# 64 places for experts 0 to 3 (nine blocks for ten), gates applied as results leave PSUM, and a reordered opening

## The reference

```python
for i in range(DEPTH):                                   # 4
    sh1, sc1, g1, sh2, sc2, g2 = adaln(c or c_ctx, w_mod[i], b_mod[i])
    x = x + g1 * mixer(rmsnorm(x, norm_mix[i]) * (1 + sc1) + sh1)
    x = x + g2 * moe(rmsnorm(x, norm_ffn[i]) * (1 + sc2) + sh2)
y = rmsnorm(x, final_norm)

def moe(h, ...):          # 16 experts in 4 groups, 1024 -> 256 -> 1024 each
    s = sigmoid(h @ w_router)        # the best group, its two best experts
    w = s[idx] / sum(s[idx])
    return sum_k w_k * (silu(h @ w_gate[e_k]) * (h @ w_up[e_k])) @ w_down[e_k]
```

## Time and profile before

| | |
|---|---|
| median of 3 runs | 1591.02 us (1586.55 to 1597.87) |
| profiled execution | 1586.19 us, its span 1584.4 us |
| TensorE busy | 1431.5 us (90%) |
| VectorE busy | 555.1 us (35%) |
| ScalarE, GpSimd busy | 372.8 us (24%), 226.8 us (14%) |
| bytes moved | 417.21 MB, 263 GB/s over the span |
| mean granted TensorE clock | 0.969 |

### The profile page before, as it was taken

The page is one execution under the profiler, slowest core; times in us unless marked ns, Lnnn a source line. Parts: engine busy times, 40 slices in busy tenths (PEclk is TensorE's granted clock), DMA queues, the critical chain, the costliest instruction groups (busy, mean ns, idle before and its releaser), DMA issues.

```text
span 1584.4 us, 26599 instructions
## 1 busy us (share of the span) xinstructions
PE 1431.5 (90%) x10752; PEld 854.6 (54%) x10752; DVE 555.1 (35%) x1362; ACT 372.8 (24%) x985; POOL 226.8 (14%) x304
## 2 busy tenths in 40 slices
PE   3999998998998998999889999989989999969983
PEld 1876685332776685333564456753337766853331
DVE  0235524211656525211622343342115256252115
ACT  0205522111214512111210342211112046121111
POOL 0100022111122022111100000222111000221112
PEclk9999998999999999999989999999999999979997
DMA  9898238999978238999857403489998870239992
GB/s 325 294 318 280 74 114 329 337 420 416 331 276 241 87 134 322 343 421 418 284 207 241 115 28 123 168 320 351 421 415 309 288 284 18 109 128 328 422 389 104
DMA packets 122788, 417.21 MB, mean 263 GB/s; under 512 B 13659, under 2 KB 55614, under 8 KB 98086
## 3 DMA queue, kind: packets, MB, share of 16 engines
q1 hardware_dynamic: 95414, 345.08, 58.0%
q0 software_dynamic: 20304, 66.47, 12.7%
q10 hardware_dynamic: 6944, 3.91, 0.8%
HBM read 389.21 MB, written 28.76 MB: 264 GB/s over the span
## 4 chain that ended last, share of the span: by engine, by line
PE 76%; DVE 8%; DMA 6%; issue 4%; ACT 3%; POOL 1%; SPq 1%; another core or an unknown queue 0%; DVEq 0%; ACTq 0%; POOLq 0%
PE bank L1847 67%; PE bank L2017 3%; PE bank L2181 2%; ACT pp L1159 2%; DMA ring<-in_w_mod 2%; DMA ids<-own_id,row_of 1%; PE bank L1904 1%; DMA hT<-h_rows,id_of 1%; DMA id_of<-ids 1%; DVE xn L1306 1%; PE bank L2193 1%; DVE gbc L1303 1%; DVE hT L1293 1%; DMA xn<-y_slots,row_of 1%; DVE xn L1316 1%
## 5 line engine op out<-in xcount | busy, mean ns | idle before, releaser
L1847 PE MATMUL bank<-ring,pp 128*32 128x512 f32 x2304 | 357.7, 597 | 17.2 <-issue 13.0
L1847 PE MATMUL bank<-ring,hT 128*128 128x256 f32 (+3 forms) x998 | 235.5, 395 | 4.3 <-DVE kT L1612 2.6
L1847 PEld LDWEIGHTS bank<-ring,hT 128*128 128x128 f32 x998 | 182.8, 193 | 53.7 <-issue 28.0
L1847 PE MATMUL bank<-work,pp 128*32 128x512 f32 x800 | 188.0, 602 | 3.2 <-DVE kT L1730 1.4
L1847 PEld LDWEIGHTS bank<-ring,pp 128*32 128x32 f32 x2304 | 97.1, 110 | 158.3 <-issue 156.6
L1847 PE MATMUL bank<-ring,xn 128*128 128x256 f32 x768 | 168.2, 380 | 0.0
L1847 PEld LDWEIGHTS bank<-ring,xn 128*128 128x128 f32 x768 | 145.0, 190 | 19.4
L1847 PE MATMUL bank<-V,pp 128*32 128x512 f32 x544 | 130.4, 605 | 0.3 <-DVE pp L1720 0.3
L1737 DVE TENSOR_TENSOR pp<-bank,pp 128x256 f32<-128x256 f32 x40 | 17.0, 425 | 297.2 <-ACT pp L1236 297.2
L1159 ACT ACTIVATE pp<-bank,neg_max 128x384 f32<-128x384 f32 x192 | 96.6, 524 | 13.3 <-DVE neg_max L1628 10.1
L907 POOL TENSOR_TENSOR x<-x,pp 128x256 f32<-128x256 f32 x48 | 38.3, 798 | 368.0 <-DVE pp L1701 368.0
(11 more groups left out here) (277 smaller groups left out, 1781.6 us busy)
## 6 DMA issues: line engine op xcount, KB each, us to landing
ring<-in_w_mod SPq DMA_DIRECT2D x70, 1024.0 KB, 6.3
ring<-in_moe_w_gate SPq DMA_DIRECT2D x40, 1024.0 KB, 7.5
ring<-in_moe_w_up SPq DMA_DIRECT2D x40, 1024.0 KB, 13.9
ring<-in_moe_w_down SPq DMA_DIRECT2D x36, 1024.0 KB, 15.9
gbc<-in_w_mod SPq DMA_DIRECT2D x17, 1024.0 KB, 8.0
work<-in_moe_w_down SPq DMA_DIRECT2D x16, 1024.0 KB
y_slots<-kT POOLq DMA_DIRECT2D x32, 512.0 KB, 8.5
work<-in_moe_w_gate SPq DMA_DIRECT2D x12, 1024.0 KB, 12.6
```

The source lines that it names most:

```text
L1847: return pe.matmul(out, lhsT, rhs, start=start, stop=stop)
```

## The change

- `SIZES`: 64 places for experts 0 to 3, then four of 96 and eight of 64: 1152 slots, 9 blocks, 7 of them stored. Experts 0 and 1 fill block 0, 2 and 3 block 1, the four of 96 blocks 2 to 4.
- DVE evicts both halves of a down projection, each multiplied with `slot_gate`: the gate row of the slot's token, which DVE makes before each block from the two gate rows and `of_cond` (whether the slot's token is a context token). `id_of` of block 0 is made for that as well. ACT's `first_half` is gone.
- `y_second` takes the place of `y_sum`. `add_rows` adds w_k * row to `x` directly, one operation of 1024 columns; `add_late` on DVE adds the late result from PSUM. `slot_gate` lies in `xn[:, 2, :]`, which is also the landing place of block 2's second row, so POOL gathers for block 2 only after the last eviction. Block 1 is finished ahead of the next layer's `norm_scale`, the rows of block 2 are added ahead of `norm_out` of block 0.
- Opening: `x_prompt` goes out first on POOL, `x_sample` on SP behind the eight `w_mod` units. ACT does the SiLU and the square of block 0 before it issues its constants. TensorE transposes block 0's norm between the two halves of the `w_mod` products; no stream waits for the constants before the first projections; the modulation's transposes use bank 6 and are no longer a job of the bank order.

With the same planner, the order and slots of the units are the same but for the first half of the experts (in layer 0: expert 7's pair ahead of the down weights of 4, and 4 in slot 6, 5 in slot 12).

```diff
-SIZES = [WIDE] * (2 * FIXED) + [NARROW] * (E - 2 * FIXED)
+LARGE = 4
+SIZES = [NARROW] * FIXED + [WIDE] * LARGE + [NARROW] * (E - FIXED - LARGE)
@@ SP, fills
                     fill_next(key)
+                    if key == ("mod", 0, 1, 3):
+                        sp.dma_start(x[:, 1:3, :], A["x_sample"][0].rearrange("(b p) d -> p b d", p=P)).then_inc(xs_in, 16)
@@ POOL
             minus_half = small[:, 56:128]
+            pool.dma_start(x[:, 0, :], A["x_prompt"][0]).then_inc(x_in, 16)
...
-            pool.wait_ge(cond_in, 16 * 7)
-            pool.dma_start(x[:, 0, :], A["x_prompt"][0]).then_inc(x_in, 16)
-            pool.dma_start(x[:, 1:3, :], A["x_sample"][0].rearrange("(b p) d -> p b d", p=P)).then_inc(x_in, 16)
...
                 for b in range(NB):
-                    for k, dst in enumerate((y_first, y_sum)):
+                    if b == 2:
+                        pool.wait_ge(y_hi, BLOCKS * (L + 1) + 1)
+                    for k, (dst, landed) in enumerate(((y_first, first_in), (y_second, second_in))):
@@ ACT, opening: these now stand ahead of load_all(act, ...)
+            act.wait_ge(cond_in, 16 * 7)
+            nc.scalar.activation(raw[0:16, 0:P], raw[0:16, 0:P], ACT.Silu).then_inc(raw_silu, 1)
+            wait_evacuated(act, "cond", "gains")
+            norm_in(0, 0)
@@ ACT, blocks
-                    if blk > 0:
-                        first_half(blk - 1)
@@ DVE, combination
-            def gather_up(L, b):
...
-            def add_gated(L, b):
...
+            def add_rows(L, b, k):
+                rows, landed = ((y_first, first_in), (y_second, second_in))[k]
+                dve.wait_ge(landed[b], 16 * (L + 1))
+                link(V_.scalar_tensor_tensor(out=x[:, b, :], in0=rows[b], scalar=wk_early[:, k, b:b + 1],
+                                             in1=x[:, b, :], op0=ALU.mult, op1=ALU.add))
+            def add_late(L, b):
+                for half in range(2):
+                    cols = slice(half * 512, (half + 1) * 512)
+                    dve.wait_ge(comb_full, 6 * L + 2 * b + half + 1)
+                    ins = V_.tensor_tensor(x[:, b, cols], x[:, b, cols], bank[COMB[b][half]][:, :], ALU.add)
+                ins.then_inc(x_moe_v, 1)
@@ DVE, gates
+            def gate_of_slots(L, blk):
+                for evacuated in (y_lo, y_hi):
+                    dve.wait_ge(evacuated, BLOCKS * L + blk + 1)
+                link(V_.tensor_scalar(slot_gate, gbc[:, 1, 0, :], of_cond[:, 0, blk:blk + 1], None, ALU.mult))
+                link(V_.scalar_tensor_tensor(out=slot_gate, in0=gbc[:, 1, 1, :], scalar=of_cond[:, 1, blk:blk + 1],
+                                             in1=slot_gate, op0=ALU.mult, op1=ALU.add))
@@ DVE, layer's start
                 norm_scale(2 * L, 0)
...
+                else:
+                    add_rows(L - 1, 2, 0)
+                    add_rows(L - 1, 2, 1)
                 for n, (what, at) in enumerate(opening(L)):
                     if what == "norm":
                         norm_out(2 * L, at)
                         if at == 0 and L > 0:
-                            add_gated(L - 1, 1)
+                            add_late(L - 1, 2)
...
-                    if n == 1 and L > 0:
-                        gather_up(L - 1, 2)
-                        add_gated(L - 1, 2)
@@ DVE, blocks
-                def second_half(blk):
+                def gated_out(blk):
...
-                    V_.tensor_copy(ys[:, blk % 2, 512:1024], bank[5][:, :]).then_inc(y_v, 1)
+                    for half, evacuated in enumerate((y_lo, y_hi)):
+                        cols = slice(half * 512, (half + 1) * 512)
+                        V_.tensor_tensor(ys[:, blk % 2, cols], bank[4 + half][:, :], slot_gate[:, cols],
+                                         ALU.mult).then_inc(evacuated, 1)
...
                     if blk > 0:
-                        second_half(blk - 1)
+                        gated_out(blk - 1)
+                    if blk == 0:
+                        dve.wait_ge(ids_ready, L + 1)
+                        conditions(0, 3)
+                        dve.wait_ge(gate_in[1], 32 * (L + 1))
+                        dve.wait_ge(h_out, 48 * (L + 1))
+                    if blk == 2:
+                        dve.wait_ge(ids_in, 16 * (L + 1))
+                        conditions(3, BLOCKS)
+                    gate_of_slots(L, blk)
...
-                second_half(BLOCKS - 1)
-                gather_up(L, 0)
-                dve.wait_ge(gate_in[1], 32 * (L + 1))
-                add_gated(L, 0)
+                if L == DEPTH - 1:
+                    add_rows(L, 0, 0)
+                gated_out(BLOCKS - 1)
+                if L < DEPTH - 1:
+                    add_rows(L, 0, 0)
+                add_rows(L, 0, 1)
+                add_late(L, 0)
@@ DVE, after further_passes
-                gather_up(L, 1)
+                add_rows(L, 1, 0)
+                add_rows(L, 1, 1)
+                add_late(L, 1)
@@ TensorE, opening
-            mods([("mod", 0, v, q) for v in range(2) for q in range(4)])
-            pe.wait_ge(const_in, 16 * 18)
...
+            mods([("mod", 0, 0, q) for q in range(4)])
+            norm_turn(0, 0)
+            mods([("mod", 0, 1, q) for q in range(4)])
@@ TensorE, blocks
-                    pe.wait_ge(y_a, n + 1)
-                    pe.wait_ge(y_v, n + 1)
+                    pe.wait_ge(y_lo, n + 1)
+                    pe.wait_ge(y_hi, n + 1)
```

More of the change, by code:

```diff
@@ L221, in homes @@
     if name == "moe_d":
-        late = (13,) if last_block(key[2]) < 7 else tuple(range(6)) + (8, 9, 10, 11) if key[2] >= E - FIXED else ()
+        late = (13,) if last_block(key[2]) < BLOCKS - 3 else tuple(range(6)) + (8, 9, 10, 11) if key[2] >= E - FIXED else ()
         return [(slot,) for slot in (6, 7, 12) + late]
@@ L298, in plan_jobs @@
     for L in range(DEPTH):
-        if L == 0:
-            order += [(("modc", L, 0), "v")]
         part = "qkv" if KINDS[L] < 2 else "lat"
@@ L434, in build @@
         y_first = [gbc[:, 0, b, :] for b in range(2)] + [work[:, 3 * KC * UC:3 * KC * UC + D]]
-        y_sum = [xn[:, b, :] for b in range(NB)]
+        y_second = [xn[:, b, :] for b in range(NB)]
+        slot_gate = xn[:, 2, :]
         late = [xn[:, k, 0:NB * LATE * P].rearrange("p (b n) -> p b n", b=NB) for k in range(2)]
@@ L1036, in norm_in @@
                 if n == 0:
-                    act.wait_ge(x_in, 32)
+                    act.wait_ge(xs_in if b else x_in, 16)
                 elif n % 2:
@@ L1082, in _ @@
                        (sink[:, 1, 0, :], A["swa_sink"][1].partition_broadcast(P))), const_in)
-            act.sem_inc(acT_ready, 1)
-            act.sem_inc(y_a, 1)
-            act.sem_inc(xT_a, 1)
-            act.sem_inc(ov_y_full, 1)
-            act.wait_ge(cond_in, 16 * 7)
-            nc.scalar.activation(raw[0:16, 0:P], raw[0:16, 0:P], ACT.Silu).then_inc(raw_silu, 1)
             mods_out([("mod", 0, 0, 3), ("mod", 0, 1, 3)])
@@ L1219, in turned_rows @@
                         .then_inc(xT_a, 1)
-                def first_half(blk):
-                    n = BLOCKS * L + blk
-                    act.wait_ge(y_full, n + 1)
-                    act.wait_ge(ys_free, n + 1)
-                    nc.scalar.copy(ys[:, blk % 2, 0:512], bank[4][:, :]).then_inc(y_a, 1)
                 turned_rows(BLOCKS * L, 0)
@@ L1347, in mod_columns @@
                 elif s == 0:
[L1348 to L1349 removed]
+                    dve.wait_ge(opening_cols, 1)
                     for v in range(2):
                         last = V_.tensor_copy(modc[:, v].rearrange("p (t h) c -> p h t c", h=2),
[L1352 removed]
+                                              bank[6][:, 2 * v * P:2 * (v + 1) * P].rearrange(
                                                   "p (h t r) -> p h t r", h=2, t=4)[:, :, :, 0:2])
[L1354 to L1355 removed]
+                    link(last)
                 else:
@@ L1543, in _ @@
                         norm_scale(2 * L, n // 3 + 1)
-                    if n == 1 and L > 0:
-                        gather_up(L - 1, 2)
-                        add_gated(L - 1, 2)
+                if L == 0:
+                    dve.wait_ge(const_in, 16 * 18)
+                    V_.tensor_copy(ident_h[:, :], ident[:, :])
+                    V_.tensor_copy(own_id[:, :], beyond[:, 0:NB])
+                    V_.tensor_copy(masks_h[:, :, :], masks[:, :, :]).then_inc(masks_ready, 1)
+                    for w in range(2):
+                        V_.tensor_scalar(sink[:, w, 1, :], sink[:, w, 0, :], -1.0, None, ALU.mult)
+                    V_.tensor_copy(start_of[:, 0:FIXED], ebase[:, 0:FIXED])
+                    link(V_.tensor_copy(cap_of[:, 0:FIXED], ecap[:, 0:FIXED]))
                 if kind < 2:
@@ L2246, in loaded @@
                 def loaded(blk):
-                    return 16 * (BLOCKS // 2 * L + blk // 2 + 1 if blk % 2 else (BLOCKS // 2 - 1) * L + blk // 2)
```

(7 more changed lines are left out.)

106 lines of the change are left out of this document (46 added, 60 removed).

## The result

The changed kernel takes 1537.9 us (median of four runs, 1533.2 to 1540.4) where the kernel before takes 1591.2 on the same chip: a ratio of 0.966, 95% interval [0.962, 0.970], 53 us less. Three later comparisons gave 0.970, 0.973 and 0.970, that is 43 to 47 us less (44 to 49 by the medians). The forecast was 26 us less, and its range ended at 1545. The profiled execution took 1539.47 us, its span 1537.7 (granted clock 0.964, before 0.969).

The account below looks back on a forecast made before the run. The weight stream was taken to end each expert stage, though TensorE is 90% busy. Experts 14.4, boundaries 2, end 6.5 and opening 3.5 made 26.4 us less, forecast 1564 us, range 1545 to 1582.

Parts of the forecast that it names:

- the boundaries: Between layers, last down projection to next first projection: 0.7 us less at each of three, 2 us in all.
- (c): End of each expert stage: the last down projection waits for both halves' eviction, 0.5 us a layer more.
- They may not be: Layer boundaries: gathered rows may land late, so x of block 0 comes at 7.5 to 8 us, not 5.6.
- Two moves eat what is won: Boundaries: block 1 finished before block 0's norm_scale, block 2's rows added before its norm_out; 0.7 us booked per boundary.
- The end: After the last layer's last down projection: 30 to 31 us for 37, 6.5 us less, from 2 to 8.
- Term (a): Expert stages: one gather and one store of 512 KB less, 1.05 MB at 421 GB/s, 2.5 us a layer.
- Term (b): Early expert stage: the hole in the weight stream filled by expert 6's pair going out earlier, about 1.6 us a layer.
- Opening: Kernel start up to the first projection: 3.5 us less booked, from -9 to +6.3.
- The token numbers: Ahead of the blocks: three more one-column matmuls for block 0, under a microsecond, hidden by the stock of weights.
- (1): Expert stages: TensorE is the bound, 48 us replaces 14.4, giving 1531 us; chance 0.08.
- (2): Opening and boundaries: the gain is eaten where work is moved, 6 us left, 1585 us; chance 0.17.
- (3): Last expert blocks: waits lower TensorE's clock, 14 us a layer, 30 us slower, 1621 us; chance 0.04.

Follow-up runs that it names:

- e3: The changed kernel with ten blocks again (96 places for experts 0 to 3), new gates and opening kept: 0.9865 of the kernel before, 21.3 us less.
- e4: The changed kernel with the opening's hunks taken out: 0.9741 of the kernel before, 40.9 us less.
- e1: The kernel before with the nine blocks alone; gates, combination and opening as before: 0.9869 of the kernel before, 20.7 us less.
- e2: The kernel before with the new opening alone: 0.9979 of the kernel before, 3.3 us less.
- e14: The changed kernel with the stores of blocks 3 and 4 made twice, 1.05 MB more a layer: 1544.8 us.
- e17: The changed kernel with experts 6 and 7 held back and expert 4's down weight ahead of 7, giving the old kernel's hole: 1549.0 us.
- e15: The changed kernel with SP holding back expert 6 alone until block 1's gate/up is done: 1542.2 us.
- e7: The changed kernel with ten blocks, the spare block given to experts 8 to 11, slots free as early: 1556.9 us, 0.9824 of the kernel before.
- e12: The changed kernel with three earlier edits (token-number writes, block 2's row adds, token-number matmuls) and x_sample behind the first projection's unit: 1535.2 us, 0.97 of the kernel before.
- e11: The changed kernel with the three matmuls for block 0's token numbers moved into a TensorE wait within block 0: 1536.6 us, 0.9706 of the kernel before.
- e8: The changed kernel loading only half of each down weight of the last eight experts: 1518.2 us.
- e16: The changed kernel loading only half of the down weights of experts 8 and 9, 1.05 MB less a layer: 1525.8 us.
- e18: The changed kernel itself, run once more as a measure: 1540.5 us, 0.9703 of the kernel before.
- e6: The changed kernel with SP holding expert 6 until after block 1's gate/up and expert 7 until after block 2's: 1562.8 us.
- e5: The changed kernel itself, run again as a measure: 1539.4 us, 0.9703 of the kernel before.
- e13: The changed kernel itself, run again as a measure: 1535.1 us, 0.9729 of the kernel before.
- e9: The changed kernel with GpSimd writing all six lists of token numbers before it waits for block 1's numbers: 1536.7 us, 0.9716 of the kernel before.

## Why the prediction was wrong

What bounds an expert stage was right, and the sign too; the terms of the gates' part were mis-sized, and the range did not reach to the result.

**What fell short most: the boundaries.** The prediction booked 2 + 6.5 us for the gates' part, less the 0.5 us a layer of (c), 6.5 in all; e3 and e4 give 18 to 20. The step that failed is what follows "They may not be", of the gathered rows: x of block 0 was put at 7.5 to 8 us after the change, with a wait for the rows in it, against 7.8 us now. But this 7.8 is layer 0 of the kernel before, a boundary at which DVE waited for no gather. The wait was set on one side alone, though the earlier trace rows shows it in the kernel before too, in layer 2. Counted on both sides the stretch takes 8.7 us with the old evictions and 6.1 with the new: 2.7 us less at each boundary, about what the work alone would give (7.8 for 5.1 with the rows in place; the prediction's own operations add up to 5.4, where it says 5.6). Of the 7.8 us, 1.5 were a wait for TensorE's late products, which now run beside the adds of rows. The move of blocks 1 and 2 ahead of block 0's norm, booked among "Two moves eat what is won", costs 0.5 us: from x of block 0 finished to the first projection it is 8.4 us in the old runs and 8.9 in the new. Over the runs with new gates the three boundaries take 54 to 58 us, over those with old ones 62 to 67: 8 us, not 2.

**The end** was put at 6.5 us. It measured 9.6 in the first pair, and 7.4 between e1 or e2 and the changed kernel. The difference is in the profiled execution of the kernel before: its last evictions begin 5.1 to 6.2 us behind the start of the last down projection in all four layers, where e1 and e2 have 3.9 everywhere and the changed kernel 3.9 to 4.3. The prediction took that delay over into the kernel after (last eviction over at 3.5 us; 1.7 measured). From there on it was close: 26.5 to 27.5 us to the end of the span, 25.7 measured. What held these evictions back in that one execution I did not isolate.

**The ninth block.** Term (a), 2.5 us a layer: e14 gave 2.4, right. Term (b), 1.6: e17 gave 2.1, e15 1.8, which the spread of the runs does not tell from 1.6. Its reading was wrong all the same, as shares say nothing of bytes; counted in bytes over four layers the term is 2.4. The hole is filled only in part, since the first of its windows stays at 245 to 319 GB/s in the changed kernel. Term (c), 0.5: right, 0.7 against 1.26 us in the rows. Together the forecast of 16 us without (c) stands against 20.7 (e1), by the interval 17 to 24.

**Not settled.** Between e3 and the changed kernel lie 22 to 26 us by the ratios of the later comparisons, 5.4 to 6.4 a layer, against 5.2 for the same edit alone; the intervals leave room for no difference. One candidate for a real one is that ten blocks leave TensorE the bound in layers 1 and 2 (e7), so that the edit relieves both resources. And of the 18 to 20 us of the gates' part the traces place 15 (boundaries 8, end 7.4), less 2 for (c); the other 5 to 7 have no place, and the intervals leave room for their being nothing.

**Opening.** 3.5 us forecast, 3.3 measured by e2, with an interval of 0.2 to 6.5. (The terms behind its "+4.8" add up to 4.5.) Its sub-steps held: ACT was free at 31.8 us (33 to 35 forecast), w_mod 3.4 us earlier (2.8 forecast). Yet one of ACT's eighteen issues took 10.09 us, from 13.08 on, so that the estimate for all of them was right without its course being foreseen. The weight of the first projection, 3.61 us late behind x_sample, was not seen; with it taken away, among other edits (e12), nothing was gained at the end.

**The token numbers** of block 0: called hidden. e11 agrees by its time. The reason given, that the stock hides them, no run shows by itself.

**Rivals.** (1), TensorE as the bound, is refuted by e1, e8 and e16. (2) did not occur. (3), waits that lower the clock, occurs in every layer and is small. In the profiled execution the four waits of 2.60 to 3.12 us are each followed by a gate/up of 8.41 or 8.77 us for 7.07 or a down of 5.34 for 3.64; layer 2's:

```profile
1130.01 5.34 PE L1867 MATMUL bank<-ring,pp 128*32 128x512 f32 x32 [2.80 <-issue]
```

That is 1.3 to 1.7 us a layer, not 14, and the stream goes on meanwhile, so that the next wait is shorter. It is no fixed price: in e18 waits of 3.11 and 3.42 us were followed by 3.64 us as ever, and in e6 waits of 2.80 to 6.42 us by work up to 2.9 us longer. Block 1's gate/up, too, took 8.5 to 8.7 us in three layers behind waits of 1.2 to 1.8 us, as it did in two layers of the kernel before (8.28 and 8.77). The Trainium skill (TensorE: Matmul & The Clock Gate, HAM oscillation) says that a loop which waits for DMA between bursts falls back to half clock; the trace of the profiled execution agrees on the fall, in four layers of four behind a wait for weights, where the kernel before showed it in one; so do e5 and e13, while e18 shows it in two.

**The range.** It took 6 us a layer, 6 of opening, 9 of boundaries and 8 at the end as its outermost corner, 47 us, and cut there. Later comparisons (43 to 47) lie at that corner, the first beyond it. The first was a favourable one, but the forecast of 26 falls short of the others too, by 16 to 21: some 4 in the ninth block, 12 to 14 in the gates' part, nothing in the opening. Had the wait stood on neither side, the boundaries would have been 2.2 us each by the prediction's own numbers (7.8 for 5.6), 6.6 for 2 and the sum 31.

## What to carry over

When a wait is put into the forecast of the kernel after, put it into the number of the kernel before as well, or take the row of before at the place where it has that wait. Count a hole in a stream in bytes per window, never in busy share, and against the traffic that will be there afterwards. Once a stream sets the end of a stage, its bytes and their starting times set the price; whether time saved ahead of such a stage is lost again is a question for a run of its own. One profiled execution can carry a delay that others of the same code do not have: read a row in more than one before a sum rests on it.

## What was not expected of the hardware

The DMA engines can show a share of 1.01 at 311 or 282 GB/s and at 423: the slow windows follow GpSimd's writes of the lists of single token numbers. e9, which puts all these writes ahead, shows that the slow window goes with them. Its windows of layer 0 from 255 us, against 311 GB/s from 268 us in the changed kernel:

```profile
255.00:267.00 12.00, 10.48 (x94) 5.59 (x93) 2.42 (x13) 0.75 (x2) 4.70 (x5) 1.00 1.00 239
267.00:279.00 12.00, 7.74 (x58) 3.02 (x62) 3.30 (x6) 2.36 (x4) 1.02 (x1) 0.86 1.01 400
```

So in layers 0 to 2 most of what is left of the hole in the changed kernel is theirs. The Trainium skill (DMA: Bandwidth & Descriptors, Specifications) asks for 512 bytes a transfer for full rate; these are numbers of 4 bytes, and the rates agree, but no run wrote them otherwise. In e9 the same writes, put ahead of a gather in GpSimd's queue, delayed it: TensorE waited 4.2 to 5.6 us for it in layers 0 to 2, where the changed kernel has up to 1.4.

After waits of 3 to 5 us for block 3's rows the granted clock of the next window was 0.72 to 0.80 in two executions (e7 above, e18's window from 291 us), and in others of the same kernel the wait was not there at all (layer 0 of the profiled execution): executions of one kernel differ by this. Layer 0's experts took 117.8 us in one execution of the changed kernel and 121.4 in another (e5).
